# Early projections in rounded pieces, with GpSimd doing the rounding, in a fused two-block kernel

## The reference

```python
h = _layernorm(x, ln_in_g, ln_in_b)
for layer in range(2):
    proj = einsum('bsd,de->bse', h, w_in[layer])          # 1024 -> 4100
    # split: A (differential attention), B (forgetting), C (stick-breaking), and gates
    y = concat([ya, yb, yc]) @ w_out[layer]
    h = _layernorm(ALPHA * h + y, ln_g[layer], ln_b[layer])
```

## Time and profile before

| | |
|---|---|
| Runs | 2116.78, 2114.75, 2114.92 us, median 2114.92 |
| Profiled execution | span 2112.8 us from the first to the last instruction, some 2.1 below the median of the runs |
| TensorE busy | 1902.5 us, 90% of the span, 6900 matmuls |
| TensorE weight loads | 1142.6 us, 54% |
| VectorE busy | 1142.6 us, 54% |
| ScalarE busy | 667.5 us, 32% |
| GpSimd busy | 25.4 us, 1% |
| Mean granted TensorE clock | 0.942 of full speed |
| Chain that ended last | PE 74%, DVE 16%, ACT 6%, issue 3%, DMA 1% |
| DMA | 135.79 MB, 64 GB/s over the span |

### The profile page before, as it was taken

The page is one execution under the profiler, slowest core; times in us unless marked ns, Lnnn a source line. Parts: engine busy times, 40 slices in busy tenths (PEclk is TensorE's granted clock), DMA queues, the critical chain, the costliest instruction groups (busy, mean ns, idle before and its releaser), DMA issues.

```text
span 2112.8 us, 19184 instructions
## 1 busy us (share of the span) xinstructions
PE 1902.5 (90%) x6900; PEld 1142.6 (54%) x6900; DVE 1142.6 (54%) x2306; ACT 667.5 (32%) x1340; POOL 25.4 (1%) x50
## 2 busy tenths in 40 slices
PE   5999999889899998989998876868999979999997
PEld 2444444434434444445333453556777868888785
DVE  4376676731999888532862352464445444444412
ACT  1123235311132344112112232335455334434411
POOL 2000000000000000000000000000000000000000
PEclk9999999999999998999998978978999979999998
DMA  6121112021211110032302011002333313332220
GB/s 219 40 80 40 41 49 67 27 80 40 80 40 40 40 70 1 1 111 72 89 20 60 12 59 30 14 18 75 90 90 102 113 41 99 100 98 84 98 100 40
DMA packets 153006, 135.79 MB, mean 64 GB/s; under 512 B 12673, under 2 KB 126977, under 8 KB 152913
## 3 DMA queue, kind: packets, MB, share of 16 engines
q1 hardware_dynamic: 149504, 124.53, 19.4%
q0 software_dynamic: 3408, 10.04, 1.6%
HBM read 130.36 MB, written 4.19 MB: 64 GB/s over the span
## 4 chain that ended last, share of the span: by engine, by line
PE 74%; DVE 16%; ACT 6%; issue 3%; DMA 1%; SPq 0%; DVEq 0%; ACTq 0%
PE proj L1262 24%; PE proj L1242 21%; PE proj L1259 11%; DVE rel_bias L1881 3%; PE proj L1239 2%; PE attn_out L1415 2%; PE score L1435 2%; PE score L1372 2%; PE proj L1435 1%; PE attn_out L1435 1%; PE turned_probs L1401 1%; DVE E L1951 1%; PE proj L1268 1%; PE turned_probs L1435 1%; DVE index_and_shared L1874 1%
## 5 line engine op out<-in xcount | busy, mean ns | idle before, releaser
L1262 PE MATMUL proj<-hT,weights 128*128 128x512 f32 x1216 | 561.9, 614 | 20.5 <-DVE raw L2135 11.4
L1262 PEld LDWEIGHTS proj<-hT,weights 128*128 128x128 f32 x1216 | 232.1, 196 | 302.6 <-issue 278.3
L1881 DVE SCALAR_TENSOR_TENSOR rel_bias<-index_and_shared,bias_deltas,rel_bias 128x128 f32<-128x128 f32 (+3 forms) x480 | 232.7, 547 | 4.3
L1242 PE MATMUL proj<-hT_high,weights_high 128*128 128x512 f32 x544 | 218.6, 402 | 7.6 <-DVE hT_low L2160 6.0
L1242 PE MATMUL proj<-hT_high,weights_low 128*128 128x512 f32 x544 | 215.8, 397 | 0.0
L1242 PE MATMUL proj<-hT_low,weights_high 128*128 128x512 f32 x544 | 215.5, 396 | 0.0
L2151 DVE TENSOR_TENSOR weights_low<-weights,weights_high 128x1024 fp32r<-128x1024 f32 (+1 forms) x122 | 135.3, 1116 | 96.4 <-ACT weights_high L1705 96.4
L1259 PE MATMUL proj<-weights,hT 128*128 128x512 f32 (+1 forms) x384 | 151.7, 553 | 0.1
L1705 ACT ACTIVATE weights_high<-weights 128x1024 fp32r<-128x1024 f32 (+1 forms) x122 | 111.5, 961 | 74.3 <-DMA weights<-in_w_ffn_down 60.5
L1242 PEld LDWEIGHTS proj<-hT_high,weights_high 128*128 128x128 f32 x544 | 103.2, 190 | 41.5 <-issue 9.5
L1453 ACT ACTIVATE tg<-proj 128x512 f32<-128x512 f32 x66 | 39.5, 599 | 267.0 <-PE proj L1242 212.2
(11 more groups left out here) (388 smaller groups left out, 2567.3 us busy)
## 6 DMA issues: line engine op xcount, KB each, us to landing
weights<-in_w_in SPq DMA_DIRECT2D x15, 2048.0 KB, 8.5
weights<-in_w_in SPq DMA_DIRECT2D x38, 512.0 KB, 4.2
weights<-in_w_ffn_gate SPq DMA_DIRECT2D x22, 512.0 KB, 4.1
weights<-in_w_ffn_up SPq DMA_DIRECT2D x22, 512.0 KB, 5.3
weights<-in_w_ffn_down SPq DMA_DIRECT2D x11, 1024.0 KB, 4.9
weights<-in_w_in SPq DMA_DIRECT2D x9, 1024.0 KB, 5.8
weights<-in_w_out SPq DMA_DIRECT2D x4, 2048.0 KB, 10.7
weights<-in_w_out SPq DMA_DIRECT2D x4, 1024.0 KB, 5.1
```

The source lines that it names most:

```text
L1242: mm = nc.tensor.matmul(ps[:, :], w_[:, k, c0:c0 + P], x_[:, k, :], start=first, stop=last)
L1262: mm = nc.tensor.matmul(ps[0:gr["M"], :], w[:, k, c0:c0 + gr["M"]], x[:, k, :], start=first, stop=last)
L1881: ins = nc.vector.scalar_tensor_tensor(o, mk, d, o, ALU.mult, ALU.add)
```

## The change

All projections on hT, the output projections of block 1 and those of HGRN become three rounded products. Only those from the latents (`qb`, `kvb`) stay fp32. Weights now come in pieces of 1024 elements a partition (512 KB): a narrow slab is 128 columns and one piece, a wide one (T groups) 512 columns and four pieces of two chunks. Each piece is loaded into a raw ring, GpSimd copies it rounded into a high ring and writes the rest over the raw piece, both in the tail too. ScalarE and VectorE no longer split weights. Outside the tail the raw ring has six slots and the high ring four, of 4352 bytes; from the latents of block 2 on four and two; in the tail nine and nine. `slab()` wraps to the start of a ring when a slab does not fit behind the last. SyncE loads a piece when the last group of what lay there is done (`free_raw`), GpSimd writes it when that holds for the high ring (`free_high`). `place_splits()` puts the splits into the list of steps, and GpSimd now walks that list, with its DMAs at their own steps. hT is kept as high and low: each `to_hT` is now read by ScalarE (high) and then VectorE (low), and `y` is split chunk by chunk before w_out. The output projection of block 1 does half 0 for all four tiles, then half 1 tile by tile with the LayerNorms; av starts with tiles 0 and 1 ahead of turning tile 3. In block 2 the index's `av` group comes first, `hi` moves ahead of `saq`, and the output projection has two halves of 512 columns in place of four quarters of 256. The forget gate takes 128 columns instead of 4. The descriptor scratch for GpSimd's DMAs is set to 4096.

```diff
-W_SLOTS = 3
+SLOT = 4 * (KD * (P + 8))
+POOL_SLOTS = 10
+PIECE = 4 * KD * P
+RAW_RING, HIGH_RING = [SLOT * i for i in range(6)], [SLOT * i for i in range(6, 10)]
+RAW_RING_2, HIGH_RING_2 = RAW_RING[0:4], [SLOT * 8, SLOT * 9]
+TAIL_RING = 9
...
+    def slab(name, K=KD, cols=P, wide=False, split=True, **kw):
+
+        raws, highs = state["rings"]
+        n = 4 if wide else 1
...
+            at = state[ring]
+            if at + n > len(on):
+                at = 0
+            sl[ring] = on[at]
+            state[ring] = (at + n) % len(on)
...
-        for t in range(NT):
-            group("T", sv, c0=0, N=512, K=KD, tile=t, dst=("V", 0), layer=l)
+        sv = slab("av", wide=True, cols=512, layer=l)
+        wide_tiles(sv, (0, 1), dst=("V", 0), layer=l)
+        turn_rows(NT - 1, **(dict(layer=l - 1) if l else {}))
+        wide_tiles(sv, (2, 3), dst=("V", 0), layer=l)
...
+        for c in range(6):
+            steps.append(("split_x", ("y", c, 1)))
+        wo = slab("wo", wide=True, cols=512, layer=l, half=0)
...
+        flush()
+        for c in (6, 7):
+            steps.append(("split_x", ("y", c, 1)))
+        steps.extend(("group", g) for g in late)
+        wide_tiles(wo, (2, 3), dst=("resid", 0), src="y", layer=l)
+        wo = slab("wo", wide=True, cols=512, layer=l, half=1)
         for t in range(NT):
...
+            wide_tiles(wo, (t,), dst=("resid", 1), src="y", layer=l)
             steps.append(("ln", (l, t)))
...
+def place_splits(steps, groups, slabs, pieces):
...
+    for i, p in enumerate(pieces):
+        for ring in ("raw", "high"):
+            p["free_" + ring] = max((slabs[o["slab"]]["last"] for o in pieces[:i] if any(
+                meets(p[ring], o[r], p["size"], o["size"]) for r in ("raw", "high"))
+                if o["slab"] != p["slab"]), default=-1)
...
+        seq = max(p["free_high"], min(p["free_raw"] + 2, slabs[p["slab"]]["first"] - 2))
...
+            for p in pieces:
+                consumed(sp, p["free_raw"])
...
+                for dst, src in piece_loads(p):
+                    sp.dma_start(dst, src).then_inc(p["loaded"], 16)
...
+                elif op == "split":
+                    p = pieces[arg]
+                    pool.wait_ge(p["loaded"], p["landed"])
+                    consumed(pool, p["free_high"])
+                    nc.gpsimd.tensor_copy(piece_view(WR, p, "high"), piece_view(W, p, "raw")).then_inc(w_high, 1)
+                    pool.wait_ge(w_high, p["nth"])
+                    nc.gpsimd.tensor_tensor(piece_view(WR, p, "raw"), piece_view(W, p, "raw"),
+                                            piece_view(WR, p, "high"), ALU.subtract).then_inc(w_low, 1)
...
+                        if s_["split"]:
+                            wh, wl = slab_view(WR, gr["slab"], "high"), slab_view(WR, gr["slab"], "raw")
+                            terms = ((wh, xh[src]), (wh, xl[src]), (wl, xh[src]))
...
-                elif op == "split":
-                    i, q, n = arg["slab"], arg["piece"], arg["cols"]
...
-                    nc.scalar.activation(half_slots(WH, slabs[i])[:, r], half_slots(W, slabs[i])[:, r], ACT.Copy).then_inc(w_high, 1)
...
-                    nc.vector.tensor_tensor(half_slots(WL, slabs[i])[:, r], half_slots(W, slabs[i])[:, r],
-                                            half_slots(WH, slabs[i])[:, r], ALU.subtract).then_inc(w_low, 1)
...
-    nc = bacc.Bacc("TRN2", target_bir_lowering=False, num_devices=1)
+    nc = bacc.Bacc("TRN2", target_bir_lowering=False, num_devices=1, dynamic_dma_scratch_size=4096)
```

More of the change, by code:

```diff
@@ L197, in group @@
         if slab is not None:
-            slabs[slab]["last"] = g
+            used(slab, g)
             if state["mid"] and kw.get("K") == KD:
@@ L430, in plan @@
             steps.append(("norm", dict(tile=NT - 1, nth=NT - 1)))
-        for t in ((NT - 2, NT - 1) if final_layer else (NT - 1,)):
-            for half in range(2):
-                group("to_hT", tile=t, half=half, layer=l, **(dict(norm=t) if final_layer else {}))
+            turn_rows(NT - 2, layer=l, norm=NT - 2)
     if not only_block1:
-        second(steps, groups, slabs, items, units, state, slab, group, weave, flush)
-    annotate(steps, groups, items, units)
-    return dict(steps=steps, groups=groups, slabs=slabs, items=items, units=units)
@@ L442, in second @@
+def second(steps, groups, slabs, items, units, state, slab, used, group, turn_rows, wide_tiles, weave, flush):
     l = DEPTH
@@ L444, in second @@
     steps.append(("angles", 0))
-    state["slots"] = [0, 1]
-    s_iq = slab("iq", K=KD, cols=512)
-    s_ak = slab("avak", K=KD, cols=392)
+    s_av = slab("avw", cols=136)
+    for t in range(NT):
+        if t == 2:
+            turn_rows(NT - 1, layer=DEPTH - 1, norm=NT - 1)
+        group("T", s_av, N=136, K=KD, tile=t, dst=("av", 0))
     for c in range(4):
-        group("F", s_iq, c0=128 * c, M=P, K=KD, dst=("qk", 4 + c), scale=1.0)
+        group("F", slab("iq", c0=128 * c), K=KD, dst=("qk", 4 + c), scale=1.0)
@@ L557, in hgrn_gate @@
     def hgrn_gate(h):
-        g = group("gate", hold["last_hgrn"] if h < 3 else hold["hgrn"], c0=256, M=P, K=KD, chunk=4 + h, layer=l,
-                  first=False, unit=None)
+        g = group("gate", slab("hgrn", c0=HG + 128 * h), K=KD, chunk=4 + h, layer=l, first=False, unit=None)
         steps.append(("gate2", g))
@@ L616, in second @@
     steps.append(("split_x", ("mix", 7, 1)))
[L617 to L619 removed]
+    for half in range(2):
+        wo = slab("wo2", wide=True, cols=512, half=half)
+        last = half == 1
         for t in range(NT + last):
             if t < NT:
[L622 to L624 removed]
+                wide_tiles(wo, (t,), dst=("resid2", half), src="mix")
             if last:
@@ L628, in second @@
                 if t:
-                    for hh in range(2):
-                        group("to_hT", tile=t - 1, half=hh, norm=NT + t - 1, parts=True)
+                    turn_rows(t - 1, norm=NT + t - 1)
     for c in range(KF):
-        sl = tail[28 + c]
-        g = group("ffgate", sl, c0=0, M=P, K=KD, ring=c % 2, parts=True)
-        split_weights()
-        group("ffup", sl, c0=128, M=P, K=KD, chunk=c, ring=c % 2, gate=g, parts=True)
-        split_weights()
+        g = group("ffgate", slab("ffg", at=128 * c), K=KD, ring=c % 2)
+        group("ffup", slab("ffu", at=128 * c), K=KD, chunk=c, ring=c % 2, gate=g)
         if 2 <= c < EARLY + 2:
```

603 lines of the change are left out of this document (284 added, 319 removed).

## The result

The changed kernel takes 2224.66 us (median of 4 runs, 2220.49 to 2227.02) against 2115.85 for the kernel before on the same chip: a ratio of 1.051 (95% interval 1.049 to 1.053), 109 us slower. The profiled execution has a span of 2221.7 us.

What follows compares the result with a forecast made beforehand. TensorE was taken to set layer 0's weave, TensorE and VectorE both nearly full in layer 1's. Terms 5 + 22 - 20 - 34 - 15 + 20 + 10 + 7 - 5 = -10, 10 us slower: 2122.8 + 2.1 = 2125, range 2050 to 2185.

Steps and rivals of the forecast that it cites:

- A: The summed case: GpSimd holds VectorE up for half of its own time; 10 us slower, 2125 us, chance 0.40.
- C: Rival: GpSimd holds VectorE up for three quarters of its time; 63 us slower, 2178 us, chance 0.22.
- Price of a piece: GpSimd's copy plus subtraction of a weight piece: 3.5 us, lower bound 2.3, upper bound 5.8.
- D: Rival: a piece costs GpSimd over 5.6 us, so it bounds the tail too; 2259 us, chance 0.07.
- Price of a product: A rounded product takes 0.2335 us; eight chunks fall from 6.86 to 5.60, 144 us of TensorE work over 114 groups.
- From held time to lost time: Weaves: layer 0 VectorE 234 beside TensorE 236 gives 243, 22 gained; layer 1 VectorE 267 against 235, 34 lost in all.
- Start: From 0 to 62 us: aq at 56.7 instead of 62.1, 5 us gained, bounds -3 and +10.
- Layer 0 output and av: 405 to 497 us: w_out's second half and av wrap in the ring, LayerNorms pace groups; 20 us lost (13 to 30).
- Layer 1 output to HGRN: Layer 1 output: same wrap, 15 us lost; second block's groups gain 20, HGRN's groups gain 10.
- Tail: hT already split, 7 us gained; output projection 5 lost; rounding taken off ScalarE and VectorE: nothing gained.
- B: Rival: GpSimd does not hold VectorE back, the engines only share time; 56 us faster, 2059 us, chance 0.28.
- E: Rival: early rounded products cost 0.286 us each, so nothing is saved and losses stay; 2223 us, chance 0.03.

Runs made afterwards that it cites:

- bench: Beside the kernel: 24 VectorE instructions of 512 elements of one kind, alone and beside GpSimd's subtraction or copy; bias form 16.4 us alone, 28.8 beside the subtraction.
- light bias: Bias table's steps cut to 8 columns in four kernels: before 2093.80 us, before with idle GpSimd pieces 2135.38, changed 2131.55, changed without weight arithmetic before the tail 2028.33.
- e7: The changed kernel with the bias table's steps cut to 8 columns: 2131.55 us, ratio 1.007 to the kernel before.
- e9: The changed kernel with no arithmetic on weights before the tail and the bias steps cut to 8 columns: 2028.33 us, ratio 0.958 to the kernel before.
- e2: The changed kernel with no rounding or remainder of weights before the tail, TensorE reading a stand-in tile: 2071.49 us, ratio 0.980 to the kernel before.
- e12: The changed kernel without the low part of the turned activations, ScalarE alone emptying those banks: 2188.01 us, ratio 1.034 to the kernel before.
- e10: The changed kernel with the second half of each layer's output projection on the first half's rounded weights: 2191.45 us, ratio 1.036 to the kernel before.
- e3: The changed kernel with ScalarE rounding each piece and GpSimd only subtracting: 2208.99 us, ratio 1.044 to the kernel before.
- e4: The changed kernel with ScalarE rounding and VectorE subtracting every piece, GpSimd doing no arithmetic: 2218.47 us, ratio 1.050 to the kernel before.

## Why the prediction was wrong

The forecast was 2125, range 2050 to 2185; measured 2224.7. The sign and the mechanism (A and C: GpSimd holds VectorE up) were right, the size was not, even C's. Of the 99 us between the loss forecast and the loss measured, 58 lie in the two weaves, 31 between layer 1's output and HGRN, 20 in the start and layer 0's output; the tail came out 10 better.

- **Price of a piece**: 3.5 forecast, 3.57 measured. D is out: it needs pieces over 5.6 on average, and the longest of all 237 took 5.5 from start to end. The upper bound of 5.8, from two memsets, said nothing of this price.
- **Price of a product**: right where it is wide: in the start 48 products take 11.19 us, 0.233 each. At N = 136 it is 0.219 at the low clock and 0.116 at the full one, no cheaper than an fp32 record.
- **How much is held**: half of GpSimd's time was taken for VectorE; 0.55 and 0.58 measured, some 9 us more in layer 0 (56 instead of 47). The half was a choice without a row, so its closeness is partly luck. C's three quarters is near the share for exposed forms beside the subtraction (bench, 0.77 and 0.86); a weave is not made of those only, and the copy holds for less (0.54).
- **From held time to lost time: the step that failed.** For layer 0 it set 234 us of VectorE beside 236 of TensorE and wrote "two full engines: 243", three per cent over the fuller one. In the trace of after the first weave has 300 us of VectorE and 297 of TensorE in 357, 19% over. At 19% the 236 would have been 281 instead of 243: 38 of the 41 us by which this term was wrong (22 gained forecast, 19.5 lost measured). In layer 1 VectorE is alone at the front, 369 of 405: forecast -34, measured -50.5. What the runs show in place of the step: each us by which VectorE grew cost 0.53 to 0.92 us of the weave (light bias: 0.29 to 0.54). Why the sum over the fuller engine is so large is known in part only. The trace of before points both ways: from 760 to 854 us TensorE was busy 83.7 and VectorE 76.7 of 94, 12% over the fuller one, but from 525 to 760, where both are fuller still (223.3 and 214.7 of 235), it is 5%. And e7's weaves are 15% over TensorE's 293 us with VectorE at 71%, e9's 7%. So two full engines by themselves do not give 19%; the traces also show held steps of up to 2.9 us in one piece and a lower granted clock in these weaves, and no run takes the three apart.
- **Start**: forecast 5 gained, 11.3 lost. The load of the first piece was put at nothing, and GpSimd waited for it:

```profile
22.16 1.04 POOL L1222 CAST weights_rounded<-weights 128x1024 fp32r<-128x1024 f32 x1 [6.18 <-DMA weights<-in_w_in]
```

The four pieces ended at 39.4 us instead of 33. They fall on the LayerNorms, whose three long steps are exposed forms (15.4 us of the arithmetic, after against e2), and VectorE's low part closes the banks (8.8, e12); e10's start shows that some 4 us of this vary with the same code. The wait of aq for its piece came as forecast (68.19 us, behind the last group of av).
- **Layer 0 output and av**: forecast 20 lost, 23.7 measured. The wrap was read rightly: a load, four pieces, 18 us of chain, 13 to 15 us by e10. The wrap of av, put at another 14, was not tried.
- **Layer 1 output to HGRN**: forecast -15 + 20 + 10 = 15 gained; measured 29.3 lost and 13.2 gained. The wrap was there again. What was overlooked are the index's values (N = 136): the 114 groups of the prediction, 20 of them in this stretch, are those of N = 512, so the values were put at no change, and they took 21.0 instead of 7.4 us, with a LayerNorm of held steps in front. The other six groups before the first index score saved 6.6 us, near the 7.6 of the price.
- **Tail**: forecast +7, -5 and 0; measured 12.2 gained. "Neither bounds it: nothing gained" was wrong by some 10 us: with ScalarE rounding (e3, e4) the tail is 677, with GpSimd 667. So ScalarE's rounding was on the path there.
- **Rivals.** B said 2059 for no hold; with no arithmetic at all it is 2071.5. That is near by luck: e2 is also without the waits for pieces, which stand in the 30 us that B had taken off for the output stages, and from layer 1's output to HGRN it gains 7.5 us where B had 25. E (no saving from the products) is out by the same run, though its 2223 lies beside the measured time.

## What to carry to other kernels

Work moved to GpSimd is not free for VectorE: in these runs VectorE grew by 0.55 to 0.58 of GpSimd's time in a mixed stretch, and back to back, with exposed forms alone, by 0.77 and 0.86 of it beside a subtraction and 0.54 beside a copy. Put such work where VectorE works from PSUM or waits. Then ask what a microsecond more on VectorE costs at the end. With TensorE at 88 to 97% of the weave it was 0.53 and 0.66 where VectorE stood at 71 and 76%, 0.85 and 0.92 where it stood at 85 and 88%, and still 0.29 to 0.54 where it stood at 55 to 61%; so the length of the fuller engine is no forecast of the stretch. Look at the widths as well: products of N = 136 lose by the split in three. Choose the number format by stage: here fp32 while the bias table fills VectorE and up to the index, rounded products after it, is 0.75% faster than the kernel before.

## What the runs showed of the hardware

- GpSimd is held as well: its subtraction of 1024 elements is 2.34 us alone, 2.67 on average beside the bias form and up to 3.23 beside a LayerNorm, once 4.40 beside a VectorE subtraction of 2048 elements (1564.86 us, changed kernel); its copy 1.04 alone, 1.38 beside the bias form and up to 2.06 in the changed kernel.
- The chain of waits can show a hold as "issue", time without a releaser, or as a long instruction; only the two timelines side by side tell it.
- In e3 VectorE's busy time in the weaves fell by 9.3 and 3.4 us when the copy left GpSimd, though in the bench the copy holds for 0.54 of its time. Whether the subtractions, then 2.55 us each, filled the place of the copies was not tried.
